# Recurrence gates computed on the four quarters of the array, and one half projection moved ahead of a head's transposes

## The reference

```
r = sigmoid(block_diag_linear(x, wa, ba))      # four blocks of 64 x 64
i = sigmoid(block_diag_linear(x, wx, bx))
log_a = -8 * r * softplus(-lambda)
h = scan(a = exp(log_a), b = sqrt(-expm1(2 * log_a)) * i * x)
y_lru = gelu(lru_g) * h
```

## Time and profile before

| | us |
|---|---|
| median of 3 runs | 2559.76 |
| profiled execution, its own time | 2560.58 |
| span of the profiled execution | 2559.3 |
| TensorE busy with matmuls | 2524.8 |
| VectorE busy | 1242.6 |
| ScalarE busy | 952.6 |

### The profile page before, as it was taken

The page is one execution under the profiler, slowest core; times in us unless marked ns, Lnnn a source line. Parts: engine busy times, 40 slices in busy tenths (PEclk is TensorE's granted clock), DMA queues, the critical chain, the costliest instruction groups (busy, mean ns, idle before and its releaser), DMA issues.

```text
span 2559.3 us, 27651 instructions
## 1 busy us (share of the span) xinstructions
PE 2524.8 (99%) x11501; PEld 2047.2 (80%) x11501; DVE 1242.6 (49%) x1771; ACT 952.6 (37%) x1297; POOL 176.7 (7%) x173
## 2 busy tenths in 40 slices
PE   8999999999999999999999999999999999999998
PEld 5777778888888888877788888888888777888886
DVE  6787666664343333456643333433333566533333
ACT  5465544442232222346432222322222455422221
POOL 1121000000011100000011100011100000011100
PEclk9999999999999999999999999999999999999999
DMA  7344123333322223321322222222223322222231
GB/s 295 139 132 136 50 83 129 103 114 100 114 99 99 93 91 113 116 88 61 99 99 99 99 99 101 100 96 99 99 99 112 111 74 83 99 99 92 92 113 66
DMA packets 41790, 267.73 MB, mean 105 GB/s; under 512 B 5593, under 2 KB 5977, under 8 KB 12098
## 3 DMA queue, kind: packets, MB, share of 16 engines
q1 hardware_dynamic: 37824, 257.44, 29.3%
q0 software_dynamic: 2592, 7.10, 0.9%
q10 hardware_dynamic: 1250, 1.42, 0.2%
HBM read 262.78 MB, written 4.21 MB: 104 GB/s over the span
## 4 chain that ended last, share of the span: by engine, by line
PE 94%; DVE 3%; ACT 1%; issue 1%; DMA 0%; SPq 0%; DVEq 0%; ACTq 0%
PE ps L420 29%; PE ps L422 28%; PE ps L421 28%; PE ps L983 1%; PE ps L703 1%; PE ps L660 1%; PE ps L720 1%; DVE wlo L1684 1%; PE ps L1019 1%; PE ps L588 0%; PE ps L590 0%; PE ps L589 0%; PE ps L1004 0%; PE ps L674 0%; DMA early<-ada_in 0%
## 5 line engine op out<-in xcount | busy, mean ns | idle before, releaser
L1684 DVE TENSOR_TENSOR wlo<-raw,whi 128x2048 fp32r<-128x2048 f32 x211 | 483.4, 2291 | 1068.5 <-ACT whi L1157 1068.4
L420 PE MATMUL ps<-ahi,whi 128*128 128x512 f32 x2272 | 895.9, 394 | 1.2 <-ACT tmp L1353 0.8
L422 PE MATMUL ps<-alo,whi 128*128 128x512 f32 x2272 | 885.3, 390 | 0.0
L421 PE MATMUL ps<-ahi,wlo 128*128 128x512 f32 x2272 | 884.6, 389 | 0.0
L1157 ACT ACTIVATE whi<-raw 128x2048 fp32r<-128x2048 f32 x211 | 403.9, 1914 | 888.1 <-PE ps L422 883.8
L420 PEld LDWEIGHTS ps<-ahi,whi 128*128 128x128 f32 x2272 | 426.6, 188 | 94.8 <-issue 7.4
L422 PEld LDWEIGHTS ps<-alo,whi 128*128 128x128 f32 x2272 | 426.4, 188 | 89.9
L421 PEld LDWEIGHTS ps<-ahi,wlo 128*128 128x128 f32 x2272 | 426.8, 188 | 89.3 <-issue 2.6
L420 PE MATMUL ps<-hhi,whi 128*128 128x512 f32 x1008 | 393.2, 390 | 3.3 <-DVE hhi L2342 3.3
L421 PE MATMUL ps<-hhi,wlo 128*128 128x512 f32 x1008 | 392.3, 389 | 0.0
L422 PE MATMUL ps<-hlo,whi 128*128 128x512 f32 x880 | 342.4, 389 | 0.0
(11 more groups left out here) (393 smaller groups left out, 1717.7 us busy)
## 6 DMA issues: line engine op xcount, KB each, us to landing
raw<-wstream SPq DMA_DIRECT2D x221, 1024.0 KB, 4.8
raw<-wstream SPq DMA_DIRECT2D x24, 512.0 KB, 5.0
early<-ada_in SPq DMA_DIRECT2D x8, 1024.0 KB, 20.8
strip<-bias_strips POOLq DMA_DIRECT2D x16, 256.0 KB, 3.8
x<-x_in SPq DMA_DIRECT2D x2, 1024.0 KB, 6.7
bias_strips<-bias_by_distance POOLq DMA_DIRECT2D x1, 2048.0 KB, 16.4
y_out<-x SPq DMA_DIRECT2D x3, 512.0 KB, 2.7
bd<-lru_in ACTq DMA_DIRECT2D x2, 256.0 KB, 3.2
```

What stands on the lines that cost most here:

```text
L420: pe.matmul(out, wh, rhi, start=start, stop=False)
L421: pe.matmul(out, wl, rhi, start=False, stop=False)
L422: return pe.matmul(out, wh, rlo, start=False, stop=stop)
L1684: dve.tensor_tensor(lo_of(u)[:], raw[r][:], hi_of(u)[:].bitcast(F32), ALU.subtract).then_inc(*inc("lo_dve", "lo", u))
```

## The change

The two block-diagonal products of `lru_gates` become four products of 64 x 64 blocks, each with 64 rows and 64 columns of the array and 512 positions. The first gate's blocks go to the quarters on the diagonal (block 0 to partitions 0 to 63 of bank 3, block 1 to 64 to 127 of bank 4), the second gate's to the other two (block 0 to partitions 64 to 127 of bank 3, block 1 to 0 to 63 of bank 4). One semaphore step tells that all are done. ScalarE applies the sigmoids in four instructions of 64 partitions; for the second gate they read one half of the partitions and write the other, so a copy of `bx` with its halves swapped is made at the kernel's start by two small copies a layer. And `quarter(23)` is issued before `turn(2, (0, 1))`, where it stood behind `turn(2, (2,))`.

```diff
@@ lru_gates, TensorE
-                    pe.matmul(bank(3), bd[l][:, f, :], W[0][:], start=True, stop=True).then_inc(*inc("gate_mm", "gate_mm", l, f, 0))
-                    pe.matmul(bank(4), bd[l][:, 2 + f, :], W[0][:], start=True, stop=True).then_inc(*inc("gate_mm", "gate_mm", l, f, 1))
+                    for gate in range(2):
+                        for block in range(2):
+                            at_, out = 64 * block, 64 * (block ^ gate)
+                            ins = pe.matmul(ps[out:out + 64, 3 + block, :], bd[l][at_:at_ + 64, 2 * gate + f, at_:at_ + 64], W[0][at_:at_ + 64, :], start=True, stop=True)
+                    ins.then_inc(*inc("gate_mm", "gate_mm", l, f))
@@ layer, TensorE
                 quarter(22)
+                quarter(23)
 
                 turn(2, (0, 1), ("gate_x", l, 0))
                 scores(3, 0)
                 turn(2, (2,))
-                quarter(23)
                 quarter(24)
@@ start, ScalarE
                 act.wait_ge(*at("lc", LAYERS - 1))
+                for to, w in ((0, 64), (64, 0)):
+                    ins = act.activation(a[to:to + 64, 24:26], lc[l][w:w + 64, LCOL["bx"]:LCOL["bx"] + 2], ACT.Copy)
+                ins.then_inc(*inc("gate_bias", "gate_bias", l))
@@ lru_gates, ScalarE
-                    act.wait_ge(*at("gate_mm", l, f, 0))
-                    act.activation(W[1][:], bank(3), ACT.Sigmoid, bias=lcol(l, "ba", f))
-                    act.wait_ge(*at("gate_mm", l, f, 1))
-                    act.activation(W[2][:], bank(4), ACT.Sigmoid, bias=lcol(l, "bx", f)).then_inc(*inc("gate_x", "gate_x", l, f))
+                    act.wait_ge(*at("gate_bias", l))
+                    act.wait_ge(*at("gate_mm", l, f))
+                    for block in range(2):
+                        to, w = 64 * block, 64 * (1 - block)
+                        act.activation(W[1][to:to + 64, :], ps[to:to + 64, 3 + block, :], ACT.Sigmoid, bias=lcol(l, "ba", f)[to:to + 64])
+                        ins = act.activation(W[2][to:to + 64, :], ps[w:w + 64, 3 + block, :], ACT.Sigmoid, bias=lsmall[l][w:w + 64, 24 + f:25 + f])
+                    ins.then_inc(*inc("gate_x", "gate_x", l, f))
```

## The result

The changed kernel takes 2566.84 us, the kernel before 2559.91 us in the same series (medians of 11 runs each): +6.9 us, ratio 1.0025, 95% interval 1.0017 to 1.0033. One of the 11 runs before took 3001.47 us; it doesn't move the median, and the ratio is that of the fast runs, not of the two medians. The changed kernel is slower, by 0.25%, a little more than the 0.2% that the prediction took as the limit of what can be told from no change. Forecast were 2565.2 us and +5.5, in a range from 2561.0 to 2567.6; the narrower range that the prediction gave the forecast itself, 2564.2 to 2566.6, was missed by 0.2.

A forecast was written before the change was run, and what follows sets the result against it. The prediction took a chain of waits that leaves TensorE at the transposes for ScalarE and VectorE as the bound. 2.03 + 0.70 = +2.73 us a layer, +5.5 over two layers, gave 2565.2 us, range 2561.0 to 2567.6.

The forecast's parts named there:

- only rows overlap: Rival at the gates' products: row halves overlap, column halves don't; +7.2 us, 2567.0 us in all; chance 0.08.
- The chain: From `turn(2, (2,))` over ScalarE and VectorE to `values(2)`: the moved quarter's delay, less the gates' saving, arrives whole, +2.03 us.
- The quarters: TensorE's products in `lru_gates`: eight passes in two waves, saving 0.70 us at tile 0 and 0.50 at tile 1.
- The rivals with less overlap: At the gates' products: rows only, 2567.0 us, chance 0.08; no overlap, 2573.2 us, chance 0.04.
- the rule of the Trainium skill: At the gates' products: up to two more weight loads would show at 0.11 us each, saving 0.5; not followed.
- The sigmoids: ScalarE in `lru_gates`: four of 64 partitions for two of 128, +1.17 us a call; `quarter(32)` 0.70 late.
- the slack: At `quarter(32)`, which waits for `z_out(18)`: it could have had the tile 0.47 us later.
- the stop at `quarter(26)`: TensorE stands 1.8 us ahead of `quarter(26)`, waiting for `z_out(17)`, which now comes behind the late transposes.
- idle time ahead of `values(2)` (1.3): Sign that the forecast is right: TensorE newly idle 1.3 us ahead of `values(2)`, waiting for `z_out(10)`.
- Cover by the moved quarter: At `scores(3, 0)`: the moved `quarter(23)` hides tile 0's ScalarE cost; without it about 0.4 us.

The follow-up runs named there:

- e5: Changed kernel plus seven filler passes of 128 x 512 between `scores(3, 1)` and `quarter(26)`: 2566.39 us, against 2559.75 for the kernel before.
- e1: Kernel before with only `quarter(23)` moved ahead of `turn(2, (0, 1))`: 2565.14 against 2559.86 us, ratio 1.0023.
- e7: Kernel before with only `turn(3, (2,))` issued ahead of `quarter(32)`: 2556.71 against 2559.75 us, ratio 0.9987.
- e3: Kernel before, full products kept, each sigmoid cut into two of 64 partitions without swapped halves: 2562.51 against 2559.86 us, ratio 1.001.
- e6: Kernel before with 20 activations added at ScalarE's end: copies 0.48 to 0.50 us apart within a group, 0.59 to 0.61 in the last group.
- e2: Changed kernel with `quarter(23)` back behind `turn(2, (2,))`, so the gates alone: 2561.63 against 2559.86 us for the kernel before, ratio 1.0008.

## Why the prediction was right, and where its sizes were off

The time alone would not have told the forecast (2565.2) from its rival *only rows overlap* (2567.0), which lies nearer to the measured 2566.84. The traces do, term by term.

- **The chain.** `turn(2, (2,))` +2.03 forecast, +2.06 measured; with the clock kept (e5) `values(2)` is 2.08 late, so it arrived whole. e1 shows the move alone doing it, e7 shows that the lever works in the other direction at the layer's other such place.
- **The quarters.** Two waves, 1.13 us a call from the first load forecast; measured 1.02 to the next load and 0.11 for that load, 1.13. That saves the forecast 0.70 at tile 0; the passes right behind lose 0.03 of it, so 0.66 and 0.53 reach the two calls of `features`, forecast 0.70 and 0.50. The rivals with less overlap are out. So is what the prediction drew from the rule of the Trainium skill ("TensorE: Matmul & The Clock Gate", section "Part 3: Packing small matmuls"), that a weight load overlaps matmuls in flight only when it goes to another row group. Two loads more should have shown and 0.5 been saved, but all eight loads are done under the first wave, although two quarters share each row group.
- **The sigmoids**, mis-sized: +1.17 a call forecast, +1.52 measured. I took the pitch of the earlier trace rows for any pair of activations; e3 and e6 show that it belongs to pairs with the same start partitions. With the slack of 0.38, where 0.47 was forecast, 1.52 - 0.38 = 1.14 is the delay of `quarter(32)` behind `mix(2)`, measured (55.63 - 37.84) - (52.20 - 35.56) = 1.15, forecast 0.70.
- **The clock**, left out: the stop at `quarter(26)` was forecast at 1.8 us, was 1.74, and I didn't ask what follows it. `values(2)` was 2.35 late in place of 2.03; e5 takes back 0.27. Most of the slow passes' price is hidden, since `values(2)` would have waited anyway. So the sign "idle time ahead of `values(2)` (1.3)" failed in the changed kernel and shows where the clock was kept, in e1's first layer and in e5 (1.2). The Trainium skill ("TensorE: Matmul & The Clock Gate", section "Part 1: The HAM clock gate (the "warmup" mystery)") says that the activity watch runs free of the program. That would fit e1's two layers; no run here shows the watch itself.
- **Cover by the moved quarter**: 0.4 at `scores(3, 0)` forecast if it were gone, 0.87 in e2 (19.64 - 18.77). That is why e1 and e2 sum to more than the change: by 2.96 + 1.39 - 3.43 = 0.92 in the second layer, and by 2.69 + 1.33 - 3.47 = 0.55 in the first, where the change lost its clock and e1 didn't.

Sum in a layer: forecast 2.73; measured 2.28 at `mix(2)` and 1.15 behind it, 3.43 at `quarter(32)`. Of the 0.70 too much, 0.45 are the sigmoids and the slack behind them, about 0.2 the clock, and the rest the chain. All three lie on the same side; no error hid another.

## What to carry to other kernels

Where an engine is busy 99% of the time, look in the chain of waits for the places at which the chain leaves it: work put ahead of such a place cost its whole length here (2.72 us for a call of 2.73, e1), and work taken from ahead of it paid (e7), even though the engine's own sum doesn't move. Cutting an instruction by partitions divided nothing on ScalarE (a sigmoid on 64 partitions took 0.69 us, as on 128): count the new instructions in full, and find what waits behind them before counting the other engine's gain. A forecast stop of TensorE needs the question what its clock does afterwards.

## What the hardware showed that I had not expected

- Products on the four 64 x 64 quarters overlap fully in float32: 8 records of 512 columns held TensorE for 1.13 us, from their first load to the first pass behind them, where 4 records of 128 x 128 took 1.83.
- Successive activations lose about 0.1 us of overlap when the start partition of input or output changes (0.48 to 0.50 against 0.59 to 0.61 for copies, 0.59 against 0.68 to 0.71 for sigmoids).
- A stop of TensorE of 1.7 us can be followed by a fall of the clock to 1.2 GHz, here over eight passes of `quarter(26)`. In the changed kernel both layers show it, in e1 one of two; the stop of 1.44 us ahead of `quarter(32)` had no fall behind it in either layer.
